# Rotary halves exchanged by a shuffle and by copies instead of matrix products, and a first block whose attention and projections follow one written order

## The reference

```python
def rope(x, pos, rot_dim, theta):
    ...
    x1, x2 = xr[..., : rot_dim // 2], xr[..., rot_dim // 2:]
    rot = jnp.concatenate([x1 * cos - x2 * sin, x2 * cos + x1 * sin], axis=-1)

def hybrid_mixer(h, w_in, attn_gn_g, ret_gn_g, w_out):
    aq, ak, av, rq, rk, rv, rg = jnp.split(h @ w_in, splits, axis=-1)
    aq = rope(heads(aq, 8, 64), pos, 16, 500000.0)
    ak = rope(heads(ak, 8, 64), pos, 16, 500000.0)
    a = dilated_attention(aq, ak, heads(av, 8, 64))
    a = a * lax.rsqrt(jnp.mean(a * a, axis=-1, keepdims=True) + RMS_EPS)
    rq = rope(heads(rq, 4, 128), pos, 128, 10000.0)
    rk = rope(heads(rk, 4, 128), pos, 128, 10000.0)
    r = retention(rq, rk * 128 ** -0.5, heads(rv, 4, 128))
    ...
    r = silu(rg) * group_norm(r)
    return jnp.concatenate([a, r], axis=-1) @ w_out
```

## Time and profile before

| | us |
|---|---|
| median of 3 runs | 2392.47 (2391.29 to 2393.3) |
| profiled execution, own time | 2392.37 |
| its span (first to last instruction) | 2390.3 |
| PE busy in it | 2316.4 (97%) |
| VectorE, ScalarE, GpSimd busy | 1289.3, 948.5, 357.4 |

### The profile page before, as it was taken

How to read it: one execution, slowest core, us unless ns; L and a number is a source line. 1 busy time by engine, 2 the same in 40 slices (tenths; PEclk the granted TensorE clock), 3 DMA queues, 4 the chain that set the end, 5 groups by cost and what they waited for, 6 DMA issues and landing times.

```text
span 2390.3 us, 29723 instructions
## 1 busy us (share of the span) xinstructions
PE 2316.4 (97%) x11942; PEld 1878.3 (79%) x11942; DVE 1289.3 (54%) x2005; ACT 948.5 (40%) x1670; POOL 357.4 (15%) x343
## 2 busy tenths in 40 slices
PE   8999999989999987999999999999999999999999
PEld 6777777768778865898988898776666788888887
DVE  4553755377666346667567767334455533642442
ACT  3234444443223235444454544345544423431331
POOL 1001142131101120233123233101111001000000
PEclk9999999999999999999999999999999999999999
DMA  5211232235564221110000001110101333233332
GB/s 198 71 62 62 93 110 80 80 132 194 182 206 157 59 84 59 58 45 27 32 22 28 19 27 54 36 54 28 35 20 55 112 107 130 88 97 97 97 97 79
DMA packets 60183, 195.71 MB, mean 82 GB/s; under 512 B 6672, under 2 KB 11536, under 8 KB 59664
## 3 DMA queue, kind: packets, MB, share of 16 engines
q1 hardware_dynamic: 60048, 193.83, 24.6%
HBM read 187.25 MB, written 6.55 MB: 81 GB/s over the span
## 4 chain that ended last, share of the span: by engine, by line
PE 89%; DVE 6%; ACT 2%; POOL 2%; issue 1%; DMA 0%; SPq 0%; DVEq 0%; ACTq 0%; POOLq 0%
PE ps L135 85%; PE ps L138 5%; DVE sb L166 2%; DVE sb L174 2%; POOL sb L166 1%; DVE r L166 1%; ACT r L147 1%; ACT sb L147 1%; DVE r L174 1%; DMA sb<-in_w_aq 0%; POOL sb L171 0%; POOL sb L157 0%; ACT L145 0%; DVE sb L171 0%; ACT sb L148 0%
## 5 line engine op out<-in xcount | busy, mean ns | idle before, releaser
L135 PE MATMUL ps<-r 128*128 128x512 f32 (+2 forms) x7176 | 1596.1, 381 | 46.0 <-DVE r L166 16.4
L135 PEld LDWEIGHTS ps<-r 128*128 128x128 f32 (+1 forms) x7176 | 1280.0, 189 | 314.0 <-issue 38.6
L135 PE MATMUL ps<-sb 128*128 128x128 f32 (+5 forms) x3764 | 692.9, 330 | 22.5 <-ACT sb L147 11.1
L166 DVE TENSOR_TENSOR r<-sb,r 128x1024 fp32r<-128x1024 f32 (+3 forms) x397 | 422.2, 1073 | 446.7 <-ACT r L147 445.9
L147 ACT ACTIVATE r<-sb 128x1024 fp32r<-128x1024 f32 (+3 forms) x445 | 381.9, 878 | 636.8 <-PE ps L135 490.0
L135 PEld LDWEIGHTS ps<-sb 128*128 128x128 f32 (+1 forms) x3764 | 507.4, 191 | 160.3 <-issue 104.3
L166 POOL TENSOR_TENSOR sb<-sb 128x512 f32<-128x512 f32 (+3 forms) x227 | 281.7, 1247 | 1521.0 <-ACT sb L147 978.8
L147 ACT ACTIVATE sb<-ps 128x256 f32<-128x256 f32 (+3 forms) x502 | 214.6, 451 | 401.4 <-PE ps L135 199.6
L166 DVE TENSOR_TENSOR sb<-ps,sb 128x512 f32<-128x512 f32 (+3 forms) x286 | 170.7, 606 | 180.7 <-PE ps L135 164.3
L174 DVE SCALAR_TENSOR_TENSOR sb<-sb 128x512 f32<-128x512 f32 (+5 forms) x240 | 234.2, 988 | 28.2 <-ACT sb L147 26.4
L147 ACT ACTIVATE sb<-sb 128x512 f32<-128x512 f32 (+4 forms) x307 | 157.3, 527 | 98.8 <-POOL sb L166 40.7
(11 more groups left out here) (25 smaller groups left out, 206.9 us busy)
## 6 DMA issues: line engine op xcount, KB each, us to landing
sb<-in_w_mlp SPq DMA_DIRECT2D x60, 512.0 KB, 3.5
sb<-in_w_mod SPq DMA_DIRECT2D x48, 512.0 KB, 4.4
sb<-in_w_qkv SPq DMA_DIRECT2D x24, 512.0 KB, 3.2
sb<-in_w_g SPq DMA_DIRECT2D x20, 512.0 KB, 4.9
sb<-in_w_u SPq DMA_DIRECT2D x20, 512.0 KB, 4.7
sb<-in_w_out SPq DMA_DIRECT2D x16, 512.0 KB, 3.4
sb<-in_w_down SPq DMA_DIRECT2D x16, 512.0 KB, 3.5
sb<-in_w_gate SPq DMA_DIRECT2D x16, 512.0 KB, 3.3
```

What stands on the lines that cost most here:

```text
L135: return QUIET if self.e is None else self.e.matmul(o, l, r, start=start, stop=stop)
L166: return QUIET if self.e is None else self.e.tensor_tensor(o, a, b, op)
```

## The change

**Swaps.** The 8 products with `permA` are gone. VectorE's shuffle, with one list of 32 partitions for every group of 32, writes the exchanged tile into TMP, and the rotation's first multiplication reads TMP in place of a PSUM bank. The 8 products with `permR` are gone as well: two ScalarE copies of 64x512 move each half to the other's partitions (`rk_sw`), and they too write the buffer that the rotation then reads. The two permutation matrices leave the table C1.

**Entry.** Keys 1 to 3 follow each other on PE, and the values go straight behind them. By the rotation of banks, without the swaps' banks, the value tiles lie in banks 2 to 5; the middle's first projection starts in banks 0 and 1. VectorE's order of rotations and `lo_to` is written anew.

**Middle.** The fixed slots and `weave` are replaced by generators, one for each kind of work (s scores, t transposes, v value products, n block ends, r projections, a on POOL), walked by a table `TURNS1`. Every instruction is the same otherwise; the products of the retention's values, which stood behind a count of turns, now stand behind `a_max` 30 and 31.

**After it.** `TURNS0` is another sequence of the same letters.

The diff, cut to its core (the generators for scores, block ends and the other engines take the bodies of `attend_*` over unchanged):

```diff
-C1 = {"permA": 128, "cosA": 512, "sinA": 512, "maskA": 512, "cosR": 512, "sinR": 512, "decay": 2048, "permR": 128}
+C1 = {"cosA": 512, "sinA": 512, "maskA": 512, "cosR": 512, "sinR": 512, "decay": 2048}
...
+SWAP8 = [(i + 8) % 16 if i < 16 else i for i in range(32)]
...
-            def swap(i):
-                b = take()
-                e.wait_ge(*at("qk_ev", i))
-                e.wait_ge(*at("c1_rot"))
-                fence(e, free[b])
-                e.matmul(P(b * 512, NT), S(O1["permA"], 128), S(QK[i][1] + QK[i][2] * NT, NT), True,
-                         True).then_inc(*up("qk_pm", i))
-                free[b], BK["qk_pm", i] = [("qk_t", i)], b
...
-            key(1)
-            swap(0)
-            key(2)
-            swap(1)
-            swap(4)
-            key(3)
-            swap(2)
-            swap(5)
+            for mt in range(1, 4):
+                key(mt)
             bs = [take() for _ in range(4)]
             values = project_rows(e, CI["w_av", 0], toks_of(HT, HL, NT, 4, "mix_lo"), bs)
-            for i in (3, 6, 7):
-                swap(i)
-                for _ in range(4):
-                    next(values)
...
-        def rotate_dve(e, tag, i, bank, o, tmp, tables, n=NT, parts=128, before=()):
+        def rotate_dve(e, tag, i, swapped, o, tmp, tables):
+
             cos, sin = tables
-            e.wait_ge(*at(tag + "_pm", i))
-            for x in before:
-                e.wait_ge(*at(*x))
-            e.tt(S(tmp, n, n=parts), P(bank * 512, n, n=parts), S(sin, n, n=parts), MU).then_inc(*up(tag + "_t", i))
-            e.tt(S(o, n, n=parts), S(o, n, n=parts), S(cos, n, n=parts), MU).then_inc(*up(tag + "_c", i))
+            e.wait_ge(*at(swapped, i))
+            e.tt(S(tmp, NT), S(tmp, NT), S(sin, NT), MU).then_inc(*up(tag + "_t", i))
+            e.tt(S(o, NT), S(o, NT), S(cos, NT), MU).then_inc(*up(tag + "_c", i))
             e.wait_ge(*at(tag + "_c", i))
-            e.tt(S(o, n, n=parts), S(o, n, n=parts), S(tmp, n, n=parts), AD).then_inc(*up(tag + "_rot", i))
+            e.tt(S(o, NT), S(o, NT), S(tmp, NT), AD).then_inc(*up(tag + "_rot", i))
...
-                rotate_dve(e, "qk", i, BK["qk_pm", i], base + mt * NT, TMP[i % 4], (O1["cosA"], O1["sinA"]))
+                e.wait_ge(*at("qk_ev", i))
+                e.wait_ge(*at("c1_rot"))
+                e.shuffle(S(TMP[i % 4], NT), S(base + mt * NT, NT), SWAP8).then_inc(*up("qk_sw", i))
+                rotate_dve(e, "qk", i, "qk_sw", base + mt * NT, TMP[i % 4], (O1["cosA"], O1["sinA"]))
...
+            rotate(0)
             lo_to(e, got, 6)
-            rotate(0)
             out_of(5)
+            rotate(1)
             lo_to(e, got, 7)
-            rotate(1)
             rotate(4)
             out_of(6)
+            rotate(2)
             c = CI["w_av", 0][0]
             lo_to(e, got, c)
-            rotate(2)
             rotate(5)
             out_of(7)
+            lo_to(e, got, c + 1)
             rotate(3)
-            lo_to(e, got, c + 1)
+            lo_to(e, got, c + 2)
             rotate(6)
-            lo_to(e, got, c + 2)
+            lo_to(e, got, c + 3)
             rotate(7)
...
-                        b = take()
-                        o = RET[i - 1][1] + (mt - 1) * NT
-                        e.wait_ge(*at("rk_ev", i - 1))
-                        for x in free[b]:
-                            e.wait_ge(*at(*x))
-                        e.matmul(P(b * 512, NT), S(O1["permR"], 128), S(o, NT), True, True).then_inc(*up("rk_pm", i - 1))
-                        free[b], BK["rk_pm", i - 1] = [("rk_t", i - 1)], b
...
-            for _ in range(16):
-                yield
+            fence(e, [("a_max", 30), ("a_max", 31)])
...
+                        o, tmp = RET[i - 1][1] + (mt - 1) * NT, TMP2[(i - 1) % 2]
+                        e.wait_ge(*at("rk_ev", i - 1))
+                        if i >= 3:
+                            e.wait_ge(*at("rk_rot", i - 3))
+                        e.act(S(tmp, NT, n=64), S(o, NT, p=64, n=64), ACT.Copy).then_inc(*up("rk_sw", i - 1, 0))
+                        e.act(S(tmp, NT, p=64, n=64), S(o, NT, n=64), ACT.Copy).then_inc(*up("rk_sw", i - 1))
...
+        def att_turn_pe(e, take):
+            for u, (qb, h) in enumerate(UNITS):
+                b = take()
+                fence(e, [("a_exp", u)] + free[b])
+                for kb in range(qb + 1):
+                    t = e.transpose(P(b * 512 + kb * 128, 128), S(SC[u % 4] + kb * 128, 128), IDN)
+                t.then_inc(*up("a_tr", u))
+                free[b], BK["a_tr", u] = [(f"a_pt{u % 2}", u)], b
+                yield
+
+        def att_value_pe(e):
+            for u, (qb, h) in enumerate(UNITS):
+                b = 6 + qb % 2
+                fence(e, [(f"a_pt{u % 2}", u), ("av_ev", 3)])
+                if h == 0:
+                    fence(e, free[b])
+                for kb in range(qb + 1):
...
+            walk_streams(TURNS1, "PE", dict(r=mix_rest_pe(e), s=att_score_pe(e, (free[2], free[3])), t=att_turn_pe(e, take), v=att_value_pe(e),
+                                            n=att_end_pe(e, take)))
...
+        TURNS1 = {
+            "PE": ("rrrsrrrsrsrstrrsrrstrrtrvtsrrrtvsrsvvtrssttrvvstrtstvvsrrsrrrstrrvvvnvtstrrvssvrrrtrtrtsrvrtvsrsstvr"
...
         TURNS0 = {
-            "PE": ("ssssssssimsssisssssiiVVVVVtVVtVVVVVtVtVVVooooooooosmoooooooKKeKKqqqqqqqeqKKxxxxKCqvvqvvKvxxvqxivxqvK"
...
+            "PE": ("sssssssmismssissssissiVVVVVVVVttVVsVVtVVtVVooooooooooooooooKKeKKqqqqqqqeqKKxxxKKxvqqvxKtxvvKvxvxvqCv"
...
-            "POOL": ("mmmmmmmmaaaaaaAaCmaCaAaCCaaCCCCaaaaaCaaACaaAaaaCfffffffffffCCfffffffffCffCaaafaaCaaAAAC"),
...
+            "POOL": ("mmmmmmmmaaaaaaaAaaAaaCaCCCCCCCCaCaaCaaCaAaaaAaCaaffffffffCfCfffffffffffffamCaCfaaaaAaAA"),
```

More of the change, by code:

```diff
@@ L195, in dma @@
         return QUIET if self.e is None else self.e.dma_start(o, i)
-def weave(*parts):
-    parts = list(parts)
-    while parts:
-        for g in list(parts):
-            if any(g is x for x in parts):
-                try:
-                    next(g)
-                except StopIteration:
-                    parts = [x for x in parts if x is not g]
 def whole(g):
@@ new lines, in att_end_pe, with att_score_dve @@
+        def att_end_pe(e, take):
+            for qb in range(4):
+                b = take()
+                fence(e, [("a_gn", qb)] + free[b])
+                for j in range(4):
+                    t = e.transpose(P(b * 512 + j * 128, 128), S(ATF[qb % 2] + j * 128, 128), IDN)
+                t.then_inc(*up("a_ct", qb))
+                free[b], BK["a_ct", qb] = [("a_y", qb)], b
+                yield
+        def att_score_dve(e):
+            for u, (qb, h) in enumerate(UNITS):
+                n, b = (qb + 1) * 128, 2 + u % 2
+                e.wait_ge(*at("a_s", u))
+                if u >= 4:
+                    e.wait_ge(*at("a_tr", u - 4))
+                if u >= 8:
+                    e.wait_ge(*at("a_exp", u - 8))
+                e.addmin(S(SC[u % 4], n), P(b * 512, n), S(O1["maskA"] + 384 - 128 * qb, n),
+                         S(AMX[u % 8], 1)).then_inc(*up("a_max", u))
+                yield
@@ new lines, in att_score_act, with att_turn_act @@
+        def att_score_act(e):
+            e.wait_ge(*at("qk_rot", 7))
+            for u, (qb, h) in enumerate(UNITS):
+                n = (qb + 1) * 128
+                e.wait_ge(*at("a_max", u))
+                e.act(S(SC[u % 4], n), S(SC[u % 4], n), ACT.Exp, scale=-1.0, bias=S(AMX[u % 8], 1),
+                      acc=S(ST[qb] + h, 1)).then_inc(*up("a_exp", u))
+                yield
+        def att_turn_act(e):
+            for u in range(1, 32, 2):
+                n = (UNITS[u][0] + 1) * 128
+                e.wait_ge(*at("a_tr", u))
+                if u >= 3:
+                    e.wait_ge(*at("a_v", u - 3))
+                e.act(S(PT[u % 3], n), P(BK["a_tr", u] * 512, n), ACT.Copy).then_inc(*up("a_pt1", u))
+                yield
@@ L877, in attend_pool, with att_end_act, att_pool @@
+        def att_end_act(e):
+            for qb in range(4):
+                e.wait_ge(*at("a_red", qb))
+                e.act(S(ST[qb] + 24, 8), S(ST[qb] + 16, 8), ACT.Ln, scale=1.0 / 64, bias=S(EPS6, 1)).then_inc(*up("a_ln", qb))
+                e.wait_ge(*at("a_ln", qb))
+                e.act(S(ST[qb] + 32, 8), S(ST[qb] + 24, 8), ACT.Exp, scale=-0.5).then_inc(*up("a_rs", qb))
+                yield
+        def att_pool(e):
             for qb in range(4):
@@ L3339, in tab @@
             s_[b + half:b + rot] = sn
-            for j in range(half):
-                pm[b + half + j, b + j] = 1
-                pm[b + j, b + half + j] = 1
-        return c_, s_, pm
-    cA, sA, pA = tab(16, 500000.0, 128, 64)
-    cR, sR, pR = tab(128, 10000.0, 128, 128)
+        return c_, s_
+    cA, sA = tab(16, 500000.0, 128, 64)
+    cR, sR = tab(128, 10000.0, 128, 128)
     log_g = np.log(1.0 - 2.0 ** (-5.0 - np.arange(4)))
```

217 lines of the change are left out of this document (75 added, 142 removed).

## The result

The changed kernel takes 2371.28 us (median of 4 runs, 2370.67 to 2372.15) against 2392.59 (2391.29 to 2393.3): 21.3 us less, ratio 0.9912, 95% interval 0.9895 to 0.9929. The forecast was 2374.5 with a range of 2367 to 2385. The profiled run took 2372.15 us with a span of 2370.4, 19.9 less than the span of before. It is the slowest of the four, 0.9 above their median.

What follows compares the result with a forecast made beforehand. PE was taken as the bound, with a VectorE and GpSimd chain deciding in the norms. Terms -6.9 + 0.6 - 1.4 - 6.9 + 0 + 0 - 2.5 - 1.0 = -18.1 us took 2392.5 to 2374.5, range 2367 to 2385.

Steps and rivals of the forecast that it cites:

- PE is the bound: Whole kernel: PE is busy 2316.4 of 2390.3 us, so work that leaves PE shortens the run unless another engine comes late.
- Rival 4: The swaps were no cost: PE's chain is bound elsewhere and gives the gain back, 2390 us; chance 0.05.
- The `permA` swaps and the shuffles: Entry: eight swaps at 0.86 us leave PE, -6.9; VectorE's shuffles make chunk 8 late, +0.6 us.
- Rival 2: VectorE becomes the bound of the entry, or ScalarE's copies delay the middle: 2380 to 2382 us; chance 0.12.
- The start of the middle: First projection no longer waits for ScalarE's copies of the value tiles: -1.4 us (-1.4 to 0).
- The `permR` swaps: Middle: eight swaps at 0.86 us leave PE for ScalarE copies that cost nothing: -6.9 us.
- The written order of the attention: Middle: PE's work is the same, only cover can change, and no wait comes out: 0, lower bound -0.3 us.
- Retention, memory, output product: 240 to 339 us: later value copies and moved transposes balance, +1.0 - 1.0: 0 (-1 to +1.5).
- The norms: Around the cross attention, squares moved behind a sum: -2.5 us (0 to -3.4); ahead of the network: -1.0 (0 to -2).
- rival 1: The middle stage (norms) gives nothing, as the chain there goes through VectorE's 1.76-us steps: 2378 us; chance 0.22.
- Rival 3: More than forecast: no wait at chunk 8, middle stage -3.4, network -2, mixer -0.3: -22, 2370 us; chance 0.06.
- The slower rival: Last query blocks: a unit's mask and exponential stand bare on PE at each pair, up to 2397.5 us; chance 0.05.

Runs made afterwards that it cites:

- e3: The kernel before with only the shuffle, the copies and the new entry; fixed slots in the middle and the old later order kept: 2376.93 us.
- e6: The changed kernel with VectorE's rotations 2, 3 and 6 in the entry moved behind rests of the weights of value chunks: 2370.6 us.
- e10: The changed kernel with five banks passed over, so the value tiles lie in banks 7, 0, 1 and 2 as before: 2374.76 us.
- e5: The changed kernel with eight unused fp32 products of 128x512 added in the middle, where the old swap products stood: 2381.84 us.
- e1: The changed kernel with five pairs of neighbouring scores separated, by transposes at four and a value product at the fifth: 2374.68 us.
- e4: The changed kernel with ten scores moved down next to the following one, giving 15 pairs of neighbouring scores: 2364.7 us.
- e9: e4 with the heads taken in the order 0, 2, 4, 6, 1, 3, 5, 7, so eight pairs read the same half of the rows: 2369.21 us.
- e2: The changed kernel with the old `TURNS0`, the order of the stages behind the mixer from the kernel before: 2371.03 us.
- e7: The changed kernel with the stream additions of tiles 2 and 5 in two norms made by VectorE in place of GpSimd: 2370.99 us.

## Why the prediction was right, point by point

**PE is the bound.** Right. 21.8 us less of PE's busy time shortened the span of the same run by 19.9. Rival 4 (the swaps were no cost) is out with e3, which gave 15.6 us.

**The `permA` swaps and the shuffles.** Right in both. The wait at chunk 8 was 0.9 us, for 0.6; a shuffle took 731 ns for the 722 of the earlier trace rows. The entry with the start of the middle: -7.7 forecast, -7.5 measured. Rival 2 (VectorE becomes the bound of the entry) is out: the shuffles cost 0.9 of the 5.8 us that they could have, and a change of VectorE's order takes even that away (e6).

**The start of the middle.** -1.4 forecast, and e10 brings that 1.4 back, at its place. The whole time of e10 went up by more (3.5), so the place is confirmed and not the time.

**The `permR` swaps.** -6.9 forecast, -6.3 measured (e3), which is nearer to the lower price of 0.77 that the prediction read beside its 0.86; put back, they cost about 0.85 each (e5). ScalarE's copies, 10.1 us of them, made PE wait nowhere.

**The written order of the attention.** This is the step that failed. It said "PE's work is the same", and took 0, with -0.3 as the lower bound; the runs show -6.1 (e3's middle against the changed kernel's). The instructions were the same, their time on PE was not: six pairs of scores overlapped. At the price of a single score they are 0.4 + 0.6 + 2 x 0.83 + 2 x 1.05 = 4.8 us (5.3 by busy time), and five of them, broken up, gave 3.9 back (e1). I had counted in the order's rows how much work stands between a step and its successor, and never asked what two instructions cost when nothing stands between them. The lower bound missed it because it was taken from rows in which no two scores are neighbours: a trace cannot price a neighbourhood that it does not have, and the bound should have been open below. The hint was in the profile of the kernel before: its rows of scores (first fence of e4) read `64*128`, half of the 128 rows. The other 1.3 of the 6.1 go with fewer changes from one kind of product to another, 104 in the trace of the changed middle and 128 in that of e3. At the 0.2 of e9 six spared changes would be 1.2, but e1 gave back only 0.3 beside its scores, so this part stays open. The bound of -0.3 was too narrow for it in either case.

**Retention, memory, output product.** 0 forecast; with e2 giving no difference, 0.

**The norms.** -2.5 and -1.0 forecast, -0.4 measured for all behind the middle. This step failed too, and rival 1 had the norms right (its time of 2378 lacks what the written order gave; e3, without it and with the old later order, took 2376.93). The prediction's own sign says the same: in the 30 us of the norms PE should have idled nearer 1 than 3.4, and it idled 5.0 (30 less the second number):

```profile
319.40:349.40 30.00, 24.97 (x101) 18.54 (x102) 26.16 (x22) 13.76 (x20) 22.56 (x18) 1.00 0.32 118
```

It reasoned from the squares on the chain, and from PE's idle time, that leaving them out would shorten the stretch. But VectorE was busy 28.1 of 29.6 us of its part, a number that the page's stretches would have given had I cut them at VectorE's first and last step and not at PE's. Here the busier of the two engines set the length of their shared chain. GpSimd's squares were work beside it: its other steps still stretch VectorE's to 1.7 us, so the way on which fewer squares would quicken VectorE brought 0.5 us of its busy time (28.13 to 27.63) and not the gain nearer to 3.4.

**The sum** came out 3 us from the measured median, and 1.8 from the difference of the spans, because the two errors had opposite signs, 5.5 too little in the middle (6.1 for the order, less 0.6 too much for the swaps) and 3 too much behind it. That was luck, and the range held for that reason as much as for the right terms.

**Rival 3 (more than forecast, 2370)** lies nearer to the measured 2371.3 than the forecast does, but not by its mechanism: the wait at chunk 8 was there (0.9), the norms did not give -3.4 and -2, and the mixer gave far more than its -0.3. Its terms as listed also add up to -20.9, which is 2371.6, and not to -22.

**The slower rival** (bare softmax steps) is out: PE waits 0.2 us in the whole middle, for a mask. Even with 15 pairs the one new wait is for a copy:

```profile
PE ps L136 <- DVE r L167: 0.9, 1, 0.9
PE ps L136 <- DVE sb L158: 0.8, 1, 0.8
```

## What to carry to other kernels

A change of order can change what instructions cost, not only what they wait for: look for small products that come to stand next to each other, and price them by pairs. Products that use one half of the rows should stand beside products that use the other half; here that was worth a whole score for nearly every pair, and 15 pairs with a small repair of VectorE's order make a kernel of 2361.6 to 2363.1 us. And before work is taken from one engine of a shared chain, read which of them is busy over the whole chain, from its own first step to its last; and before an added instruction is used as a price, look at what else it moves, here a bank and a pair.

## What the runs showed of the hardware

Two fp32 products of 64 rows, on partitions 0 to 63 and 64 to 127 and into different banks, of 512 columns each, start 0.006 us apart and take 1.06 us together, one alone 1.05; on the same half they take 1.91 (the changed kernel, e4, e9). The overlap needs them next to each other in PE's list: with a group of transposes or a value product between them it is gone (e1). And an operation's busy time on VectorE in the norms is 1.7 us beside a GpSimd step and 0.7 without, and moving two GpSimd steps to VectorE made VectorE less busy (27.63 to 26.86 us, e7). A shuffle of 128x512 took 731 ns on VectorE, and a copy of 64x512 to the other 64 partitions 630 ns on ScalarE.
